# Second output projection: last two products tile by tile, splits ahead, first weight roundings on ScalarE

## The reference, cut to what matters

```python
mixed = jnp.concatenate([rms_norm_2(attn, attn_out_norm[l]),
                         rms_norm_2(sgu, sgu_out_norm[l])], axis=-1)
y = mixed @ w_out[l]                       # 1024 x 1024 @ 1024 x 1024
x = x + rms_norm_2(y, post_mix_norm[l])
h = rms_norm_2(x, pre_ffn_norm[l])
f = (jax.nn.silu(h @ w_gate[l]) * (h @ w_up[l])) @ w_down[l]
```

## Time and profile before

| | us |
|---|---|
| median of 3 runs | 2117.76 (2116.98 to 2122.84) |
| profiled execution | 2117.39 |
| its span | 2115.6 |
| TensorE busy | 2011.5 (95%) |
| VectorE busy | 1334.1 (63%) |
| GpSimd busy | 956.7 (45%) |
| ScalarE busy | 844.4 (40%) |
| mean granted TensorE clock | 0.978 of full speed |

### The profile page before, as it was taken

The page is one execution under the profiler, slowest core; times in us unless marked ns, Lnnn a source line. Parts: engine busy times, 40 slices in busy tenths (PEclk is TensorE's granted clock), DMA queues, the critical chain, the costliest instruction groups (busy, mean ns, idle before and its releaser), DMA issues.

```text
span 2115.6 us, 27416 instructions
## 1 busy us (share of the span) xinstructions
PE 2011.5 (95%) x10009; PEld 1665.5 (79%) x10009; DVE 1334.1 (63%) x1759; ACT 844.4 (40%) x1349; POOL 956.7 (45%) x566
## 2 busy tenths in 40 slices
PE   7999999999999999989998999875999999999997
PEld 6888888888887778768887698664888888878885
DVE  7886777665547555964422443797665565556977
ACT  5444444444420044650203766356333233324443
POOL 1345545323234397623542100776645555535552
PEclk8999999999999999999999999997999999999998
DMA  9223322211112152331112001122333233247344
GB/s 285 65 75 110 119 70 91 57 30 30 51 51 80 43 191 86 134 125 52 50 30 80 1 1 37 34 100 70 105 112 97 88 119 104 96 163 248 100 135 154
DMA packets 178924, 193.96 MB, mean 92 GB/s; under 512 B 9799, under 2 KB 122904, under 8 KB 178842
## 3 DMA queue, kind: packets, MB, share of 16 engines
q1 hardware_dynamic: 172420, 178.53, 26.6%
...
## 4 chain that ended last, share of the span: by engine, by line
PE 78%; DVE 11%; ACT 5%; issue 4%; POOL 2%; ACTq 0%; DMA 0%; SPq 0%; DVEq 0%; POOLq 0%
PE psum L1488 7%; PE psum L1490 7%; PE psum L1489 7%; PE psum L958 6%; PE psum L960 6%; PE psum L959 6%; PE psum L1119 3%; PE psum L1556 3%; PE psum L1399 3%; PE psum L1558 3%; PE psum L1557 3%; PE psum L980 3%; PE psum L979 3%; PE psum L978 3%; PE psum L1276 2%
## 5 line engine op out<-in xcount | busy, mean ns | idle before, releaser
L754 POOL TENSOR_TENSOR w_hi<-w_raw,ones 128x1024 fp32r<-128x1024 f32 x60 | 149.3, 2489 | 485.4 <-PE psum L960 357.2
L958 PE MATMUL psum<-h_hi,w_hi 128*128 128x512 f32 x704 | 284.2, 404 | 0.0
L960 PE MATMUL psum<-h_hi,w_lo 128*128 128x512 f32 x704 | 274.8, 390 | 0.0
L959 PE MATMUL psum<-h_lo,w_hi 128*128 128x512 f32 x704 | 274.3, 390 | 0.0
L1588 ACT ACTIVATE arena<-psum 128x1024 f32<-128x1024 f32 (+7 forms) x135 | 100.8, 750 | 218.9 <-PE psum L960 133.7
L757 POOL TENSOR_TENSOR w_lo<-w_raw,w_hi 128x1024 fp32r<-128x1024 f32 x60 | 166.0, 2767 | 4.7
L958 PEld LDWEIGHTS psum<-h_hi,w_hi 128*128 128x128 f32 x704 | 132.4, 188 | 28.4 <-issue 2.6
L959 PEld LDWEIGHTS psum<-h_lo,w_hi 128*128 128x128 f32 x704 | 132.4, 188 | 28.3 <-issue 2.6
L960 PEld LDWEIGHTS psum<-h_hi,w_lo 128*128 128x128 f32 x704 | 132.1, 188 | 28.5
L1556 PE MATMUL psum<-w_hi,h_hi 128*128 128x512 f32 x308 | 121.5, 395 | 8.2 <-DVE h_lo L3027 5.1
L1557 PE MATMUL psum<-w_lo,h_hi 128*128 128x512 f32 x308 | 120.9, 392 | 0.0
...
## 6 DMA issues: line engine op xcount, KB each, us to landing
w_raw<-w_in SPq DMA_DIRECT2D x64, 512.0 KB, 3.8
...
w_raw<-w_gate SPq DMA_DIRECT2D x22, 512.0 KB, 3.9
w_raw<-w_up SPq DMA_DIRECT2D x22, 512.0 KB, 5.1
arena<-ada_w SPq DMA_DIRECT2D x16, 512.0 KB, 7.2
arena<-w_out SPq DMA_DIRECT2D x16, 512.0 KB, 5.8
out_T<-arena SPq DMA_DIRECT2D x16, 512.0 KB, 5.7
```

The costliest lines, as they stand in the source:

```text
L958: pe.matmul(o, wh, xh, start=(k == 0), stop=False)
L959: pe.matmul(o, wh, xl, start=False, stop=False)
L960: return pe.matmul(o, wl, xh, start=False, stop=(k == KT - 1))
```

## The change

The splits of steps 24 to 27 stand ahead in the order `Q_SPLITS`, in places of their own (`h_hi` rows 4 to 7, `h_lo` rows 4 to 7, `qa_last`). P3 and P2 run tile by tile: for each token tile the four steps of P3, then the four of P2. The sums, squares, rows and rounds of tiles 0 to 3 are written per tile of 1024 elements, not per half; seven rounds in place of six. ScalarE makes the high parts of the gate/up weights A11, A12, S2, S1. The B11 and B21 transposes wait for the C12 sum of tile 3.

```diff
+Q_ALL = QN - 2 * QJ
+Q_SPLITS = (list(range(11)) + [26] + list(range(11, 14)) + [27] + list(range(14, 17)) + [24, 17, 25] + list(range(18, 24)))
+Q_POS = {n: a for a, n in enumerate(Q_SPLITS)}
...
-    return Q_HI + (Q_FIRST[n, of_b] if n < 4 else 2 * n + 1 + of_b)
+    return Q_HI + (Q_FIRST[n, of_b] if n < 4 else 2 * Q_POS[n] + 1 + of_b)
...
         def q_a(n):
+            if n in (24, 25):
+                return [h_hi[:, 2 * n - 44 + e, HALF:] for e in range(2)]
             x = qa_ring[:, n % 4] if n < QN - 2 else qa_last[:, n - (QN - 2)]
             return [x[:, e, :] for e in range(2)]
...
-            return [h_lo[:, n % 4, e * HALF:(e + 1) * HALF] for e in range(2)]
+            r = n % 4 if n < 24 else n - 20
+            return [h_lo[:, r, e * HALF:(e + 1) * HALF] for e in range(2)]
...
                 hi, lo = w_slot(name)
                 raw = product_raw(name, 0)
-                TT(hi.rearrange("p (a n) -> p a n", n=P), raw.rearrange("p (a n) -> p a n", n=P), half_scale, ALU.mult).then_inc(gw_round, 1)
+                if q >= 4:
+                    TT(hi.rearrange("p (a n) -> p a n", n=P), raw.rearrange("p (a n) -> p a n", n=P), half_scale, ALU.mult).then_inc(gw_round, 1)
                 pool.wait_ge(gw_round, q + 1)
                 TT(lo, raw, hi.bitcast(F32), ALU.subtract).then_inc(gw_ready, 1)
...
                 if n == 2 * QJ:
                     pe.wait_ge(o_p1, Q_P10 + 4)
-                elif j == 0 and n > 2 * QJ:
-                    pe.wait_ge(o_sums, Q_C0 + O_C[{3: "X", 4: "U3", 5: "U4", 6: "C21"}[n // QJ]] + 4)
-                if n < QN - O_TAIL:
+                elif j == 0 and 2 * QJ < n <= Q_ALL:
+                    pe.wait_ge(o_sums, Q_C0 + O_C[{3: "X", 4: "U3", 5: "U4"}[n // QJ]] + 4)
+                if n < Q_ALL:
                     q_operands(n)
                     for t in range(4):
                         mm = q_out(n, j, t)
                     mm.then_inc(o_step, 1)
-            for n in range(QN - O_TAIL, QN):
-                q_operands(n)
             for t in range(4):
-                for n in range(QN - O_TAIL, QN):
+                for n in range(Q_ALL, Q_ALL + QJ):
+                    if t == 0:
+                        q_operands(n)
+                    mm = q_out(n, n % QJ, t)
+                mm.then_inc(o_step, 1)
+                pe.wait_ge(o_sums, Q_C0 + O_C["C21"] + t + 1)
+                for n in range(Q_ALL + QJ, QN):
                     mm = q_out(n, n % QJ, t)
                 mm.then_inc(o_step, 1)
 
...
 
             pe.wait_ge(xn_done, 2 * NT + 4)
-            pe.wait_ge(o_sums, Q_C0 + O_C["C12"] + 4)
+            pe.wait_ge(o_sums, Q_C0 + O_C["C12"] + 7)
             transpose_half(4, 1, range(4))
-            pe.wait_ge(o_sums, Q_C0 + O_C["C11"] + 1)
+            pe.wait_ge(o_sums, Q_C0 + O_C["C12"] + 2)
             pe.wait_ge(gw_ready, 1)
             for k in range(4):
...
 
             def q_hi_a(n, name, j):
-                if n >= 4:
+                if 4 <= n < 24:
                     act.wait_ge(o_step, Q_STEP + n - 3)
+                if n in (24, 25):
...
-                if n in (24, 25):
-                    for t in (2 * (n - 24), 2 * (n - 24) + 1):
-                        out_square("C21", t, 4 + t, NT + 4 + t, 1)
-                if n == 26:
-                    out_root(0, 1)
-                    out_x(0, 1)
-            out_root(1, 1)
-            out_xn(1, 0, 1)
-            out_x(1, 1)
+
+            def q_root(r):
+                act.wait_ge(ms_done, M_RES[1] + r + 1)
+                q = ms_pair[r % 2][:, slice(*Q_ROUND[r])]
+                A(q, q, ACT.Sqrt).then_inc(sqrt_done, 1)
+
+            def q_xn(r, t, at):
+                act.wait_ge(rstd_done, M_RES[1] + r + 1)
+                A(Y[:, t, :], XR[:, t, :], ACT.Identity, scale=rstd_pair[r % 2][:, at:at + 1]).then_inc(xn_done, 1)
+
...
+            def q_square(t):
+                act.wait_ge(o_sums, Q_C0 + O_C["C12"] + 2 * t + 2)
+                act.wait_ge(ysq_done, 24 + 2 * t)
+                A(page(26), Y[:, t, :], ACT.Square, accum_out=ss[:, NT + t:NT + t + 1]).then_inc(ysq_done, 2)
...
+            def gu_first(name):
+                raw = a_raw(name, 0) if name[0] == "A" else s_raw[name]
+                if name[0] == "A":
+                    act.wait_ge(raw_in[0], 16 * (U_DOWN // 4 + 1))
+                    act.wait_ge(ob_lo, Q_BLO + QN)
+                else:
+                    act.wait_ge(s0_done, S0_BASE + {"S1": 1, "S2": 3}[name])
+                copy(w_slot(name)[0], raw).then_inc(gw_round, 1)
+
+            mul = lambda k: col("pre_ffn_norm_2", k)
             for t in range(4):
-                out_square("C12", t, 8 + t, t, 1)
...
+                out_square("C21", t, 4 + t, NT + 4 + t, 1)
+            q_root(0)
+            q_x(4)
+            q_x(5)
+            q_square(0)
+            gu_first("A11")
+            gu_first("A12")
+            q_root(1)
+            q_xn(1, 5, 3)
+            q_x(6)
+            q_x(7)
+            q_root(2)
+            q_xn(2, 7, 3)
+            q_square(1)
+            q_root(3)
+            q_x(0)
+            q_x(1)
+            q_square(2)
+            gu_first("S2")
+            gu_first("S1")
+            q_root(4)
+            q_xn(4, 1, 3)
+            q_x(2)
+            q_square(3)
             take_b11(mul, range(0, 2))
-            out_root(3, 1)
+            q_root(5)
+            q_xn(5, 2, 2)
             take_b11(mul, range(2, 4))
-            out_square("C11", 2, 14, NT + 2, 1)
-            out_square("C11", 3, 15, NT + 3, 1)
-            take_b11(mul, range(4, 6))
-            out_x(2, 1)
-            out_root(4, 1)
-            out_xn(4, 2, 1)
-            take_b11(mul, range(6, KT))
-            out_x(3, 1)
-            out_root(5, 1)
-            out_xn(5, 3, 1)
+            q_x(3)
+            q_root(6)
+            take_b11(mul, range(4, KT))
             take_b22(mul)
...
-                dve.wait_ge(o_step, Q_STEP + ((p + 1) * QJ if p < NPR - 1 else QN - O_TAIL + t + 1))
+                dve.wait_ge(o_step, Q_STEP + ((p + 1) * QJ if p < 5 else Q_ALL + 2 * t + p - 4))
...
-            for n, name, j in q_steps():
+            for n, name, j in q_splits():
...
-                if 22 <= n < 24:
-                    out_row("C22", 2 * (n - 22), 2 * (n - 22), 1)
-                    out_row("C22", 2 * (n - 22) + 1, 2 * (n - 22) + 1, 1)
-                if n in (23, 24):
-                    q_product(4, 2 * (n - 23))
-                    q_product(4, 2 * (n - 23) + 1)
-                if n == 24:
-                    first_half(4, 4, 1)
-                    out_row("C21", 0, 4, 1)
-                    out_row("C21", 1, 5, 1)
-                    out_ms(0, 0, None, 1)
-                if n == 25:
-                    out_rstd(0, 0, None, 1)
-                    out_row("C21", 2, 6, 1)
-                    out_row("C21", 3, 7, 1)
-            out_ms(1, 1, 0, 1)
-            out_rstd(1, 1, 0, 1)
...
+            def q_rstd(r, y=(), xn=None):
+                m, rs = ms_pair[r % 2], rstd_pair[r % 2]
+                dve.wait_ge(sqrt_done, M_RES[1] + r + 1)
+                cs = slice(*Q_ROUND[r])
+                dve.reciprocal(rs[:, cs], m[:, cs]).then_inc(rstd_done, 1)
+                dve.wait_ge(rstd_done, M_RES[1] + r + 1)
+                if xn is not None:
+                    TS(Y[:, xn, :], XR[:, xn, :], rs[:, 2:3], None, ALU.mult).then_inc(xn_done, 1)
+                for a, t in enumerate(y):
+                    dve.wait_ge(x_in[t], 16 * 3)
+                    dve.wait_ge(ycp_done, 16 + (t + 1 if t >= 4 else 8 + 2 * t + 2))
+                    STT(XR[:, t, :], Y[:, t, :], rs[:, 2 - len(y) + a:3 - len(y) + a], XR[:, t, :], ALU.mult, ALU.add).then_inc(res_done, 1)
+
+            def q_row(t):
+                dve.wait_ge(ysq_done, 24 + 2 * t + 2)
+                TT(Y[:, t, :], Y[:, t, :], POST_ROW, ALU.mult).then_inc(ycp_done, 2)
+
+            mul = lambda k: col("pre_ffn_norm_2", k)
             for t in range(4):
-                q_product(5, t)
-            out_ms(2, None, 1, 1)
...
-            first_half(0, 12, 1)
-            mul = lambda k: col("pre_ffn_norm_2", k)
+                q_product(4, t)
+            out_row("C22", 2, 2, 1)
+            out_row("C22", 3, 3, 1)
+            first_half(4, 4, 1)
+            out_row("C21", 0, 4, 1)
+            out_row("C21", 1, 5, 1)
+            q_ms(0, y=(4, 5))
+            q_rstd(0, y=(4, 5))
+            out_row("C21", 2, 6, 1)
+            out_row("C21", 3, 7, 1)
+            q_product(5, 0)
             q_product(6, 0)
+            q_ms(1, y=(6, 7), x=(4, 5))
+            q_rstd(1, y=(6, 7), xn=4)
+            q_product(5, 1)
+            q_row(0)
+            q_ms(2, x=(6, 7))
+            q_rstd(2, xn=6)
             q_product(6, 1)
-            out_row("C11", 0, 12, 1)
-            out_row("C11", 1, 13, 1)
-            out_ms(3, 2, None, 1)
+            q_row(1)
+            q_ms(3, y=(0, 1))
```

(25 more changed lines are left out.)

53 lines of the change are left out of this document (35 added, 18 removed).

## The result

The changed kernel took 2123.23 us (median of 7 runs) against 2116.98 us (7 runs, 2115.44 to 2122.84) for the kernel before. One of its seven runs took 3203.69 us at a mean granted clock of 0.586; the ratio, 1.0024 with a 95% interval of 1.0012 to 1.0035, leaves it out, and the other six have a median of 2122.62 us (2120.92 to 2126.45). So it is slower by 5 us, a difference under 0.3% that the interval still separates from none. I had forecast 2117.5 in a range up to 2123.0: 2123.23 lies just outside and 2122.62 just inside, so on which side of that end the time fell is chance. That the change costs about 5 us where I forecast none is not.

The account below looks back on a forecast made before the run. GpSimd bounds to 1366, then TensorE to 1413.63, then VectorE and ScalarE handing work to each other until 1452. Step 23 +2.9, low parts -2.7, blocking -8, idle +7.7 sum to -0.1 us: 2117.5, range 2112.5 to 2123.

Parts of the forecast that it names:

- steps 11 to 19: TensorE's stretch from step 11's start, moved to 1366.20; held at 25.2 us as before, so ending at 1391.3.
- rival 3: Clock at its low level after TensorE idles 17 us before the transposes; 1.3 us each for two groups, 2120; chance 0.09.
- The delay from step 11: GpSimd's first early low part, 1.73 us, moves TensorE's step 11 from 1364.47 to 1366.20.
- marker: Start of the transposes for B12 and B22, 1451.86 before; forecast at 1451.8, a shift of -0.1 us.
- Step 23 and the start of the chain: VectorE's low part of step 23 ends at 1396.0, 2.9 us later; the first reciprocal comes at 1403.8.
- The ledger: Each engine's list in the new order at its rows' durations, starting when engine and releaser are done; marker at 1451.8.
- Blocking against idle time: VectorE up to the marker: about 8 us less blocking beside GpSimd, against 7.7 us of new idle time.
- The tail: From ScalarE's first take of the B11 and B21 transposes, at 1435.1, to the marker at 1451.8.
- rival 2: Late release of P3's banks delays ScalarE's first take, tail stays 23.6 us; marker +6.9 us, 2124.4; chance 0.10.
- Tile by tile worth nothing: P3 and P2 on TensorE: the chain does not wait for their results, so earlier arrival gains nothing by itself.
- ScalarE's roundings: Four operations, 5.1 us or more, leave GpSimd; ScalarE gets four copies, 2.4 us; gain counted with the early splits' in blocking.
- my later theory: Follow-up theory: roundings worth 1.8 us of VectorE time lost beside GpSimd, against 1.2 us added ahead of ScalarE's second root.

Follow-up runs that it names:

- after2: The changed kernel once more, unchanged, for a second profile on another chip; ratio 1.0022 to the kernel before.
- e2: The kernel before with GpSimd computing the low part of step 11 twice; ratio 1.0009 to the kernel before.
- e1a: The changed kernel with only the splits of steps 26 and 27 moved back, around step 13; ratio 1.0010 to the kernel before.
- e7: The changed kernel with all four extra splits later, ScalarE's second root and scaling earlier, VectorE's first two C22 rows later; ratio 1.0007 to the kernel before.
- e3: The changed kernel with P3 for all four tiles, then P2 for all four; ratio 1.0020 to the kernel before.
- e4: The changed kernel with ScalarE's four roundings given back to GpSimd; ratio 1.0032 to the kernel before.
- e6: The kernel before with only the four roundings given to ScalarE; ratio 0.9985 to the kernel before.

## Why the prediction was wrong

**The step that failed** is "TensorE took 1389.68 - 1364.47 = 25.2 us for steps 11 to 19, so it ends step 19 at 1391.3". I moved GpSimd's and TensorE's lists forward and did not lay VectorE's inserted low parts beside the sums on which TensorE waits. In the kernel before the U3 sums end just when step 16 needs them. In the changed one TensorE waits 1.71 us for them without a slow stretch and 2.02 with one. From the start of step 11 to that of step 20 TensorE took 25.86 us before, 28.08 in after2 and 30.67 in the changed kernel's first profile; counted from step 10, step 20 comes 3.9 us later (after2), not 1.7. To that come the slow stretches: 2.6 us more in the profile of the changed kernel. Behind step 20 the forecast held much better: it implies 1.8 us less than before, and there were 1.1 less (after2) and 1.3 (first profile). The prediction's rival 3 had the clock, but put it behind the transposes, at the place where TensorE idles longest, and not at step 11, where the change itself makes an idle time.

**The delay from step 11** was right in size: 1.7 us, as forecast. e2 shows that such a delay arrives at the marker whole in the kernel before. In the changed one it adds nothing, since step 16 waits for the U3 sums anyhow: 21.35 us behind step 10 with the delay (after2) and without it (e1a). What it does bring is an idle time of 2.08 us, behind which the clock can fall.

**Step 23 and the start of the chain.** Step 23's low part ends at 1399.9 (1396.0 forecast), and the first reciprocal comes at 1409.58 (1403.8). The further 1.9 us are two small operations that took 1.25 and 1.24 (1404.60 and 1408.07) beside GpSimd's weight sums, where e7 shows 0.16 for the first of them (1403.95). The ledger charged blocking to large operations only, though its own text named the small ones. Each of the two ends with the GpSimd operation beside it, 1404.09 + 1.74 and 1407.67 + 1.62.
The Trainium skill, SBUF — State Buffer, section "SBUF: two separate sides", says that the lock on the shared port pair is held for a whole instruction. The rows at 1404.60 and 1408.07 agree in kind: what such a wait costs goes by the length of GpSimd's instruction and not by that of VectorE's.

**Blocking against idle time** was the heart of the sum, and it came out nearly right. I compare its terms with what VectorE did from the end of step 23's low part to the marker, nearly the same work in every profile: the change moves four low parts ahead of it, merges rows and has one round more. That end came 32.01 us behind step 10 before, 37.06 in after2 and 38.54 in the first profile.

| term | forecast | after2 | first profile |
|---|---|---|---|
| end of step 23's low part | +2.9 | +5.05 | +6.53 |
| VectorE busy (52.61 us before) | -10.7 | -9.75 | -8.81 |
| VectorE idle (6.16 us before) | +7.7 | +7.52 | +7.54 |
| marker | -0.1 | +2.82 | +5.26 |

The forecast's -10.7 are its -2.7 for the four low parts and its -8 for blocking, which is 12 - 4.4 = 7.6 rounded up. Its +7.7 is over an idle time before that I took as 5 us, where the trace has 6.16. The increase in idle time was right to 0.2 us. The work saved was 0.9 us too much, and 1.9 in the first profile, where both small operations are blocked. The rest of the miss, 2.2 us and 3.6, is the late start: the step named above. The two columns on VectorE in the table of experiments begin at a fixed time instead, so a delay moves earlier work into them: they show 5.4 us less work and 8.2 us more waiting for after2, with the same sum.

**The tail** was right. From the first take at 1441.25 to the marker it is 16.2 us, 16.7 forecast, 23.6 before. So rival 2, the late release of P3's banks, came with about its sum (+6.9 forecast, +5.3 measured) by another mechanism: the transposes do start late, at 1439.66, but the tail behind them did shorten as the forecast had it.

**Tile by tile worth nothing** was right (e3). **ScalarE's roundings** I never priced by themselves; they are worth 2.6 us at the marker in e4 and 2.9 in e6 (3.2 in e6's time), more than the 1.8 us of my later theory. Between 1390 and 1452 the residuals cost the same in e6 as before (12.8 us for eight); what was freed is three row products (5.09 to 2.97 us) and one scaling (1.43 to 0.75), and they stand on VectorE's chain.

**The numbers.** The marker's shift of +5.3 us in the profile and the +5 us of the ratios agree; without slow stretches the marker's shift is +2.8, inside the 3 us that I had named for the forecast. I gave slower by more than 0.3% a chance of 0.10 and put the upper end of the range 5.5 us above the forecast; a second mechanism on that side, with TensorE's own sums late, would have moved it.
